# Moving the value products of an attention half behind other work on TensorE

## The reference, cut to what matters

```python
z = rms_norm(x, g_mix) @ w_in                    # q (8 heads x 64) | k (2 x 64) | v (2 x 64) | GLU value | GLU gate
q, k = rms_norm(q, g_q), rms_norm(k, g_k)        # per head
u = a * sigmoid(b)                               # GLU, then a causal depthwise convolution of width 31
s = q @ k.T * 64 ** -0.5 - slope * distance      # banded: two past chunks of 64 and the own one
pr = softmax(concat([s, sink]))[..., :-1]
o = pr @ v                                       # the value products
c = silu(layer_norm(conv(u))) @ w_pw + b_pw
x = x + concat([rms_norm(o, g_oa), rms_norm(c, g_oc)]) @ w_out
# then a mixture of 32 experts (top 2), and a gated per-layer embedding
```

## Time and profile before

| what | value |
| --- | --- |
| median of 3 runs | 1279.09 us (1278.03 to 1282.56) |
| the profiled execution, its time | 1281.99 us |
| its span, from the first to the last instruction | 1280.2 us |
| mean granted clock of TensorE | 0.990 of full speed |
| PE busy | 1231.3 us, 96% of the span |
| PEld busy | 1030.6 us, 81% |
| DVE busy | 958.0 us, 75% |
| ACT busy | 716.0 us, 56% |
| POOL busy | 407.1 us, 32% |
| attention stage around the change | 180 us to 345 us of the span |

### The profile page before, as it was taken

The page is one execution under the profiler, slowest core; times in us unless marked ns, Lnnn a source line. Parts: engine busy times, 40 slices in busy tenths (PEclk is TensorE's granted clock), DMA queues, the critical chain, the costliest instruction groups (busy, mean ns, idle before and its releaser), DMA issues.

```text
span 1280.2 us, 18408 instructions
## 1 busy us (share of the span) xinstructions
PE 1231.3 (96%) x6415; PEld 1030.6 (81%) x6415; DVE 958.0 (75%) x968; ACT 716.0 (56%) x882; POOL 407.1 (32%) x397
## 2 busy tenths in 40 slices
PE   6999988999999999879999999999999999999998
PEld 5887977778778888468888888888888888877886
DVE  5223957688784224849999999999999999986662
ACT  4213324756572122338777777777777777774221
POOL 1000006565142000025444454444544445431000
PEclk9999997999999999989999999999999999999999
DMA  7831001100245111459999999999999999975521
GB/s 259 169 66 34 4 17 59 34 17 12 67 153 182 66 69 47 152 204 377 397 383 379 374 372 368 381 368 386 386 400 394 395 400 398 397 304 198 163 88 61
DMA packets 79568, 287.45 MB, mean 225 GB/s; under 512 B 32864, under 2 KB 35616, under 8 KB 54174
## 3 DMA queue, kind: packets, MB, share of 16 engines
q1 hardware_dynamic: 69294, 268.93, 56.5%
q0 software_dynamic: 10224, 17.85, 3.7%
HBM read 275.60 MB, written 30.60 MB: 239 GB/s over the span
## 4 chain that ended last, share of the span: by engine, by line
PE 54%; DVE 3%; DMA 1%; issue 1%; ACT 0%; POOLq 0%; POOL 0%; SPq 0%; DVEq 0%; ACTq 0%
PE ps L465 17%; PE ps L463 17%; PE ps L464 16%; PE ps L1931 4%; DMA mem<-h_rows,mem 1%; PE ps L1938 1%; DMA mem<-y_rows 0%; DVE whl L444 0%; PE ps L1953 0%; DVE mem L1768 0%; DVE mem L1870 0%; DVE mem L1869 0%; DMA y_rows<-mem 0%; PE ps L2293 0%; DVE mem L1760 0%
## 5 line engine op out<-in xcount | busy, mean ns | idle before, releaser
L444 DVE TENSOR_TENSOR whl<-mem,whl 128x2048 fp32r<-128x2048 f32 (+2 forms) x216 | 488.9, 2267 | 31.2 <-ACT whl L1199 24.5
L463 PE MATMUL ps<-whl,ahl 128*128 128x512 f32 x1136 | 450.1, 396 | 4.8 <-DVE ahl L444 2.4
L1199 ACT ACTIVATE whl<-mem 128x2048 fp32r<-128x2048 f32 x202 | 387.4, 1919 | 95.9 <-PE ps L465 95.9
L465 PE MATMUL ps<-whl,ahl 128*128 128x512 f32 x1136 | 438.2, 386 | 0.0
L464 PE MATMUL ps<-whl,ahl 128*128 128x512 f32 x1136 | 437.3, 385 | 0.0
L463 PEld LDWEIGHTS ps<-whl,ahl 128*128 128x128 f32 x1136 | 216.0, 190 | 46.0 <-DVE whl L444 4.4
L465 PEld LDWEIGHTS ps<-whl,ahl 128*128 128x128 f32 x1136 | 214.8, 189 | 43.6
L464 PEld LDWEIGHTS ps<-whl,ahl 128*128 128x128 f32 x1136 | 215.6, 190 | 39.4
L900 POOL DMA_INDIRECT y_rows<-mem x35 | 92.4, 2639 | 291.9 <-DVE mem L1808 291.1
L785 POOL TENSOR_SCALAR mem<-mem 128x1 f32<-128x1 f32 (+2 forms) x68 | 20.5, 301 | 397.3 <-ACT mem L976 365.7
L444 DVE TENSOR_TENSOR ahl<-ps,ahl 128x512 fp32r<-128x512 f32 (+1 forms) x106 | 88.3, 855 | 71.0 <-ACT ahl L1324 33.2
(11 more groups left out here) (231 smaller groups left out, 1340.4 us busy)
## 6 DMA issues: line engine op xcount, KB each, us to landing
mem<-in_w_e_gate SPq DMA_DIRECT2D x66, 1024.0 KB, 7.4
mem<-in_w_e_up SPq DMA_DIRECT2D x66, 1024.0 KB, 7.4
mem<-in_w_e_down SPq DMA_DIRECT2D x66, 1024.0 KB, 7.6
mem<-in_x_prompt SPq DMA_DIRECT2D x24, 512.0 KB, 3.5
mem<-y_rows SPq DMA_DIRECT2D x16, 512.0 KB, 4.8
mem<-in_w_in SPq DMA_DIRECT2D x4, 1024.0 KB, 11.7
mem<-in_w_out SPq DMA_DIRECT2D x4, 1024.0 KB, 6.4
h_rows<-mem SPq DMA_DIRECT2D x8, 512.0 KB, 2.6
```

The lines of the kernel that those rows point to most:

```text
L444: return which.tensor_tensor(out, full, hi.bitcast(F32), ALU.subtract)
L463: nc.tensor.matmul(out, act_hi, whl[:, 0, w_at], start=first, stop=False)
L465: return nc.tensor.matmul(out, act_lo, whl[:, 0, w_at], start=False, stop=last)
L1199: nc.scalar.activation(whl[:, 0, slot * CH:(slot + 1) * CH], raw[c], ACT.Copy).then_inc(s_mhi, jobs)
```

## The change

The iteration of the loop on PE issues the same instructions in another order. From tile 4 on, `attend(t, 0)` comes after the second `turn_conv` of the iteration. For tiles 1 to 3, which have no `turn_conv`, the last projection chunk `qkv(t + 1, 3)` is split: its first block stays where it was, its second block moves behind `score(t, 1)` and ahead of `attend(t, 0)`. The programs of the other engines stay as they are.

```diff
                 if t >= 4:
                     turn_conv(2 * t - 8)
-                qkv(t + 1, 3)
+                qkv(t + 1, 3, (0, 1) if t >= 4 else (0,))
                 prob_transpose(t, 0)
                 score(t, 1)
-                attend(t, 0)
                 if t >= 4:
                     turn_conv(2 * t - 7)
+                else:
+                    qkv(t + 1, 3, (1,))
+                attend(t, 0)
```

## The result

The changed kernel takes 1297.12 us in the median of six runs (1292.07 to 1302.01), the kernel before 1280.03 us (1278.03 to 1285.82) in the runs taken beside it and ahead of it. The ratio is 1.0125, with a 95% interval of 1.0102 to 1.0148: slower, by 16.0 us on the ratio (13 to 19 us). The forecast, 12.2 us more and a median of 1291.3 us in a range of 1285 to 1298 us, had the sign and the place right.

The account below looks back on a forecast made before the run. PE was taken as the bound throughout. 4.5 (tile 1) + 2.8 + 2.4 (tile 2) + 2.1 + 2.4 (tile 3) - 2.0 (tiles 4 to 7) = 12.2 us, added to 1279.1 us, gave 1291.3 us; range 1285 to 1298 us.

Parts of the forecast that it names:

- Tiles 4 to 7: Value products behind the convolution unit: it fills their 0.54 us wait, 0.5 us gained per tile, 2.0 us in all.
- later steps might give back a part: Tiles 4 to 7: later steps of DVE's chain, such as the next input's low part, may reduce the gain; lower end nothing.
- The wait in tiles 1 to 3: Value products wait for a copy queued on ACT behind the squares: 4.5, 2.8 and 2.1 us later in tiles 1, 2, 3.
- terms at the full clock: Delay of the value products without clock loss: 2.8 us in tile 1, 2.8 in tile 2, 2.6 in tile 3.
- is not late against PE: Tiles 1 to 3: q and k normalising shifts by as much as the value products, so `qk_turned` adds no delay.
- third rival: Tiles 1 to 3: waits merely moved and filled if ACT copied before the squares; about 1278 us, no measurable change; chance 0.03.
- The clock: Tiles 2 and 3: one new fall to 0.50 each, priced 3.7 us, 2.4 us left after a later wait covers part.
- rival of early falls: Tiles 2 and 3: clock drops already ahead of `prob_transpose`, another 3.2 us per tile; +18.6 us, 1297.7 us; chance 0.08.
- against the profiled execution's own time: Whole kernel: 12.2 us added to the profile's 1281.99 us gives 1294.2 us; the profile stood 2.9 us above the median.
- No new falls: Rival for tiles 2 and 3: clock does not fall anew; +7.9 us, 1287.0 us; chance 0.34, including only one fall.
- the gaps are split by work: Tiles 2 and 3: argument for no new clock falls, +7.9 us, chance 0.34: work divides the gaps; 1.2 us gaps were harmless.
- The clock staying up in tile 1: Rival: the moved block prevents tile 1's old fall, -1.3 us for that tile; +2.1 us in all, 1281.2 us; chance 0.07.

Follow-up runs that it names:

- e9_warm_all: Changed kernel with identity products (14, 9, 2 ahead of the transposes, 10 ahead of the value products) filling PE's waits in tiles 1 to 3: 1285.68 us, ratio 1.0036.
- e1_late_tiles: Kernel before with only the edit for tiles 4 to 7, tiles 1 to 3 left as they were: 1277.93 us, ratio 0.998.
- e3_copy_first: Changed kernel with ACT's copy of the transposed exponentials put ahead of the squares in tiles 1 to 3: 1288.48 us, ratio 1.0059.
- e13: Kernel before, nothing changed, profiled a third time: 1280.46 us.
- e12: Changed kernel, nothing altered, profiled a second time: 1292.09 us.
- e11: Kernel before, nothing changed, profiled a second time: 1287.52 us.
- e6_tile2_alone: Kernel before with the projection's second block moved behind the scores in tile 2 only: 1288.67 us, ratio 1.0053.
- e2_early_tiles: Kernel before with only the edit for tiles 1 to 3, tiles 4 to 7 left as they were: 1297.04 us, ratio 1.0119.
- e8_warm_2_3: Changed kernel with identity products filling PE's waits in tiles 2 and 3 alone, tile 1 left as changed: 1289.40 us, ratio 1.0067.
- e4_kept_busy: Changed kernel with more identity products (24, 16, 6 ahead of the transposes, 18 ahead of the value products) in tiles 1 to 3: 1289.97 us, ratio 1.0070.

## Why the prediction was right, and where it was short

**Tiles 4 to 7.** Forecast 2.0 us gained, measured 1.75 us (0.27, 0.31, 0.67, 0.50) against the first profile of before, and alone it is a ratio of 0.998. Right in mechanism and size, for that profile. The falls behind the 0.54 us waits, about 1.6 us in four of five profiles with the old order, were not in the rows, and the forecast knew nothing of them. The price for tiles 4 and 5 was nearer to 0.3 than to 0.5 us, as the forecast allowed when it said that later steps might give back a part.

**The wait in tiles 1 to 3.** The squares start right behind the moved block, the copy stands behind them, the value products 2.43 us later: each step is in the trace. With the clock kept up the three iterations of e9_warm_all are 3.0, 2.6 and 3.2 us longer than those of e1_late_tiles (20.46, 20.05, 20.66), 8.8 us in all. The forecast's terms at the full clock are 2.8 for tile 1, 2.8 for tile 2 and 2.6 for tile 3, 8.2 us. Right. Its sentence that `qk_turned` "is not late against PE" was right for the changed kernel, but hid that this chain was as late as the other; only e3_copy_first showed it. For this reason the third rival, that a copy ahead of the squares would bring 1278 us, was wrong in itself: it is 1288.5 us.

**The clock.** Here lies what was missing. The forecast took a fall in tiles 2 and 3 at 2.4 us each and the loss in tile 1 as given. By the rows, the changed kernel's first profile lost 150.58 - 140.17 = 10.4 us to the clock, the sum of e9_warm_all being 140.17 us, and its second 7.6 us. Tile 2 lost 3.6 us (26.28 against 22.63), since the clock was down for the scores and the moved block also. The forecast had priced that only in its rival of early falls, though the earlier trace rows show slow scores in tile 1 of before (1.94 us, where the earlier trace rows have 1.14 us). Tile 3 lost 1.5 us or nothing. Tile 1 lost 5.2 and 4.1 us. The first profile is the usual case: five of the six runs of the changed kernel have a mean clock of 0.981 or 0.982 like it (0.981), and one, 1292.07 us, has 0.987 like the second. Against the one profile from which it was worked out the forecast was near in each place: 4.9, 6.2 and 4.7 us for tiles 1, 2 and 3, where it had 4.5, 5.2 and 4.5.

**What before itself lost.** The step that fell short is "against the profiled execution's own time": 12.2 us was added to the median as it was to the profile. But the profile of before carried a fall in tile 1 that cost 3.3 us (23.77 against 20.46) and that does so in some runs of before and not in others; the forecast treated it as fixed. The profile that is nearest to the median, e13 with 1280.46 us, has 20.66 us there. Against that profile, 150.58 - 134.95 is 15.6 us and e12's 147.82 gives 12.9 us, with the fall of 1.6 us in its tile 7 counted in 134.95; the runs' ratio says 16.0 us. So the mechanism was right, and the clock term was the one mis-sized: 4.8 us of new falls, where against a run of before without the fall in tile 1 they come to 8 to 10 us.

How often the fall in tile 1 comes, the profiles and the mean clocks tell together. Of five profiles of that code three had the costly one (before, e11 and e6_tile2_alone), and e13 and e1_late_tiles had not. Of the 63 runs of before that were taken beside the experiments, 23 have a mean clock of 0.991 or less, as the first profile (0.990) and e11 (0.988) have, and a median of 1284.7 us; 40 have 0.992 or more, as e13 has (0.993), and a median of 1279.2 us. So the median run of before is without it, as far as the mean clock of a run can tell. As an estimate from all these numbers: 8.8 us of waits, 10.4 us of clock, less 1.8 us for tiles 4 to 7, less what before loses on average to its own falls, 1.2 us in tile 1 (3.3 us in 23 of 63) and 1.3 us in tiles 4 to 7 (1.6 us in four of five), make about 15 us, and 16.0 us (13 to 19) were measured.

**The rivals.** By the number alone the rival of early falls, 1297.7 us, is the nearest to the 1297.12 us measured. That is luck: its two terms of 3.2 us came to about 1.2 us in tile 2 and nothing in tile 3, and the 3.3 us that the profile of before had lost in tile 1, and its median run had not, make up for them.

No new falls: e9_warm_all is that case, made on purpose, but it does not come by itself; tile 2 lost clock in each of the four profiles in which its block was moved, ACT kept its order and the waits were left idle (after, e2, e6 and e12, all 26.2 to 26.3 us). That the gaps are split by work, as the forecast says for this rival, did not keep the clock up: PE stood idle for 2.18 to 2.21 us and again for 2.48 us, with 5.0 us of work between, and the granted clock was down to 0.57 to 0.64 over 4 us in each of the four. The clock staying up in tile 1 did not happen in the changed kernel's two profiles nor in e2_early_tiles and e8_warm_2_3, which share its tile 1 (0.60, 0.59, 0.70 and 0.57 from 212 to 216 us); with the copy first (e3_copy_first) it did (1.00 from 210 to 232 us). Early falls did happen in tile 2, at about a third of the 3.2 us that I had put on them (3.6 us in all against the 2.4 us of a late one).

## What to carry to other kernels

Before a piece of work is moved into a gap, look up who waits for its last instruction: a block that raises a semaphore is no free filler. Here two chains on other engines started from it, and one of them ran through the very instruction that the gap was waiting for. A filler must be work whose end nobody needs soon, as the convolution unit was. And where PE stands idle for a microsecond or two several times in a row, compare more than one profile, since the clock may have been lost in one run and not in the next, as it was in tile 1 of e11 (2.21 us idle, 0.50 from 216 to 220 us) and not of e1_late_tiles (2.12 us idle, 1.00), and a forecast that adds to a single profile inherits its luck. The mean granted clock of the unprofiled runs says how common the profiled case is.

## What the runs showed of the hardware

The granted clock fell from 1.00 to 0.50 behind short waits (0.50 from 252 to 256 us in the first profile of the changed kernel, behind 2.48 us), and behind the same wait in one run and not in another. Ahead of tile 1's transposes PE stood idle for 1.98 us (e13, fell, and the transposes themselves were slow), 2.12 us (e1_late_tiles, stayed), 2.21 us (e11, fell), 2.33 us (e6_tile2_alone, fell), 2.42 us (first profile, fell) and 3.04 us (e3_copy_first, stayed, with no further wait until the value products were done). So in these six the length of the one wait did not decide it. Behind the waits of 0.53 or 0.54 us in tiles 4 to 7 it fell four times in twenty. Products of the identity with itself, at 0.22 us each (36 records in 4.02 us for 18 of them), held it at 1.00 from 210 to 345 us in e4_kept_busy and e9_warm_all, where they stood in the waits of tiles 1 to 3.
